# Delta rule of a recurrent mixer on quarter-array blocks: one block for the tiles, one solve of eight units, a scan with joined query and key products, and a merge in token rows

## The reference, cut to what matters

```python
def run_gdn(q, k, v, g, beta, s0, emit):        # chunks of 64 tokens, heads of 128
    gc = jnp.cumsum(g, axis=-1)
    decay = jnp.exp(jnp.where(lower, gc[..., :, None] - gc[..., None, :], -jnp.inf))
    lmat = jnp.where(strict, einsum(k * beta, k) * decay, 0.0) + jnp.eye(CHUNK)
    rhs = concatenate([v * beta, k * beta * exp(gc)])
    u0, kcd = triangular_solve(lmat, rhs, unit_diagonal=True)
    kd = k * exp(gc_last - gc);  gl = exp(gc_last)
    attn = einsum(q, k) * decay;  qd = q * exp(gc)     # latent chunks only
    def step(s):
        u = u0_i - kcd_i @ s
        s_new = s * gl_i + kd_i.T @ u
        o = qd_i @ s + attn_i @ u                      # latent chunks only
y_gdn = head_rmsnorm(o_forward + o_backward, gdn_norm_w) * silu(z)
y_gla = head_rmsnorm(o_gla, gla_norm_w) * silu(g)
```

## Time and profile before

| | us |
|---|---|
| median of 3 runs | 2598.92 (2583.86 to 2602.16) |
| the profiled execution, device time | 2598.43 |
| its span | 2596.6 |

### The profile page before, as it was taken

How to read it: one execution, slowest core, us unless ns; L and a number is a source line. 1 busy time by engine, 2 the same in 40 slices (tenths; PEclk the granted TensorE clock), 3 DMA queues, 4 the chain that set the end, 5 groups by cost and what they waited for, 6 DMA issues and landing times. The chain is left out here.

```text
span 2596.6 us, 34628 instructions
## 1 busy us (share of the span) xinstructions
PE 2331.0 (90%) x14344; PEld 2015.8 (78%) x14344; DVE 1617.0 (62%) x2449; ACT 860.4 (33%) x1198; POOL 0.2 (0%) x4
## 2 busy tenths in 40 slices
PE   4999999989999999899958995878799987878998
PEld 2998998866799899669957885878589976345997
DVE  1878877254687887468754556676467734444545
ACT  2344443034434544243435322320143411112442
POOL 0000000000000000000000000000000000000000
PEclk9999999979999999999979997988699989789999
DMA  8765886200688688258841120000077743001551
GB/s 324 292 247 190 324 323 260 84 15 29 256 327 313 259 323 323 85 218 327 321 168 49 65 84 31 1 1 1 0 281 304 304 157 130 1 0 65 212 197 53
DMA packets 65739, 450.64 MB, mean 174 GB/s; under 512 B 8023, under 2 KB 9240, under 8 KB 12696
## 3 DMA queue, kind: packets, MB, share of 16 engines
q1 hardware_dynamic: 65624, 449.09, 45.2%
HBM read 448.01 MB, written 1.05 MB: 173 GB/s over the span
## 5 line engine op out<-in xcount | busy, mean ns | idle before, releaser
L460 PEld LDWEIGHTS banks<-ffn_h_split,ffn_weights_split 128*128 128x128 f32 x7392 | 906.5, 194 | 25.3 <-DVE ffn_weights_split L533 11.7
L460 PE MATMUL banks<-ffn_h_split,ffn_weights_split 128*128 128x256 f32 x7392 | 910.4, 285 | 17.5 <-DVE ffn_h_split L550 17.4
L678 DVE TENSOR_TENSOR ffn_weights_split<-weight_ring,ffn_weights_split 128x2048 fp32r<-128x2048 f32 x224 | 511.9, 2287 | 236.7 <-ACT ffn_weights_split L593 236.5
L593 ACT CAST ffn_weights_split<-weight_ring 128x2048 fp32r<-128x2048 f32 x224 | 425.5, 1903 | 169.0 <-PE banks L475 168.8
L475 PE MATMUL banks<-ffn_weights_split,ffn_hidden_split 128*128 128x512 f32 x1512 | 354.7, 390 | 0.0
L475 PEld LDWEIGHTS banks<-ffn_weights_split,ffn_hidden_split 128*128 128x128 f32 x1512 | 279.9, 188 | 55.5
L641 DVE CUSTOM_DVE_ANT_0 weight_ring<-weight_ring,first_arena,cols 128x1024 f32<-128x1024 f32 x200 | 245.3, 1279 | 0.0
L564 ACT ACTIVATE ffn_arena<-banks 128x256 f32<-128x256 f32 x154 | 59.1, 384 | 526.8 <-PE banks L460 526.8
L796 PE MATMUL banks<-h,weight_ring 128*128 128x256 f32 x544 | 123.5, 392 | 7.6 <-PEq L84 7.6
L796 PEld LDWEIGHTS banks<-h,weight_ring 128*128 128x128 f32 x544 | 107.2, 197 | 24.0 <-issue 8.4
L627 DVE TENSOR_TENSOR ffn_arena<-banks,ffn_arena 128x256 f32<-128x256 f32 x154 | 64.7, 420 | 49.0 <-ACT ffn_arena L564 49.0
(11 more groups left out here) (327 smaller groups left out, 2431.0 us busy)
## 6 DMA issues: line engine op xcount, KB each, us to landing
weight_ring<-in_weights SPq DMA_DIRECT2D x407, 1024.0 KB, 4.9
first_arena<-in_norm_rows SPq DMA_DIRECT2D x12, 512.0 KB, 6.7
first_arena<-in_c_rows SPq DMA_DIRECT2D x4, 512.0 KB, 5.7
h<-in_ctx SPq DMA_DIRECT2D x1, 1024.0 KB
first_arena<-in_x SPq DMA_DIRECT2D x1, 1024.0 KB
first_arena<-in_ctx_rows SPq DMA_DIRECT2D x1, 1024.0 KB
x<-in_x_rows SPq DMA_DIRECT2D x1, 1024.0 KB
recurrent_arena<-in_ctx SPq DMA_DIRECT2D x1, 1024.0 KB, 4.9
```

Of the source, the lines that this page charges most:

```text
L460: last = nc.tensor.matmul(bank[:, half * T:half * T + T], w[:, x, sl], hs[:, k, y, :], start=(k == 0 and x + y == 0), stop=(k == DT - 1 an ...
L593: nc.scalar.copy(wsplit[:, c % S, 0, :], raw).then_inc(self.split_hi.sem, 1)
L678: nc.vector.tensor_tensor(wsplit[:, c % S, 1, :], core.wbuf[:, (self.first + at(c)) % NSLOT, :], wsplit[:, c % S, 0, :].bitcast(F32), ALU. ...
```

## The change

- GLA merge: the sums over the head are made with one column of ones, so they stand with tokens on partitions (128x8 for all heads). Root and reciprocal are taken of 128x8, spread over the features by matmuls (`rstd` broadcast against the identity), and applied as two products of 128x512.
- `gdn_tiles` does factors and all four tiles in one block, with two sets of banks and two sets of rows.
- `gdn_solve` runs once, on eight units. X, W and the products are stored as 128x256: the 64x64 blocks of a head's two chunks lie one above the other, and every product is eight matmuls of 64x64 blocks, those of chunk one in the upper left quarter of the array, those of chunk two in the lower right. Units follow each other in slots; `product(n)` and `change(n - 3)` alternate. X and W of a unit share one bank and one subtraction. The keys scaled for the state (`kte`) are made by ScalarE here.
- `gdn_scan`: keys and queries of a latent chunk stand side by side (`kq`), so one product gives both `kcd @ s` and `qd @ s`; `attn @ u` is added in the same bank, with tokens on partitions. The scaling L2032 is gone. Context steps have an additional matmul of 128x256 with the identity whose result nobody reads. The output of the two directions is put together in token rows, normed there, turned by eight transposes, and gated. `ab_merge` is gone.

```diff
             pe.wait_ge(state.sem, state.base + 16)
             for hd in range(NG):
                 pe.wait_ge(msquared.sem, msquared.base + hd + 1)
-                last = nc.tensor.matmul(core.ps[hd // 2][:, (hd % 2) * T:(hd % 2) * T + T], core.ones[:, :],
-                                        b["msq"][:, hd, :], start=True, stop=True)
+                for t in range(TT):
+                    last = nc.tensor.matmul(core.ps[0][:, 2 * hd + t:2 * hd + t + 1], b["msq"][:, hd, t * P:t * P + P],
+                                            core.ones[:, 0:1], start=True, stop=True)
+            last.then_inc(sums.sem, 1)
+            pe.wait_ge(msteps.sem, msteps.base + 1)
+            for hd in range(NG):
+                for t in range(TT):
+                    last = nc.tensor.matmul(core.ps[1 - hd // 2][:, (hd % 2) * T + t * P:(hd % 2) * T + t * P + P],
+                                            b["rstd"][:, 2 * hd + t:2 * hd + t + 1].broadcast_to([P, P]), core.ident[:, :],
+                                            start=True, stop=True)
                 if hd % 2:
-                    last.then_inc(sums.sem, 1)
+                    last.then_inc(spread.sem, 1)
...
+            act.wait_ge(sums.sem, sums.base + 1)
+            nc.scalar.activation(b["root"][:, :], core.ps[0][:, 0:2 * NG], ACT.Sqrt, scale=1.0 / P, bias=core.rms_eps)\
+                .then_inc(mact.sem, 1)
...
+            step, z = Steps(dve, msteps), b["lg"]
+            dve.wait_ge(mact.sem, mact.base + NG + 1)
+            step(nc.vector.reciprocal(b["rstd"][:, :], b["root"][:, :]))
             for hd in range(NG):
-                dve.wait_ge(mact.sem, mact.base + NG + hd + 1)
-                step(nc.vector.reciprocal(msq[:, hd, :], msq[:, hd, :]))
-                step(nc.vector.tensor_tensor(msq[:, hd, :], o_of(hd), msq[:, hd, :], ALU.mult))
-                step(nc.vector.scalar_tensor_tensor(z[:, hd, :], msq[:, hd, :], core.col("gla_norm_w")[:, 0:1], z[:, hd, :],
-                                                    ALU.mult, ALU.mult))
+                last = nc.vector.scalar_tensor_tensor(z[:, hd, :], o_of(hd), core.col("gla_norm_w")[:, 0:1], z[:, hd, :],
+                                                      ALU.mult, ALU.mult)
+            step(last)
+            for a in range(2):
+                dve.wait_ge(spread.sem, spread.base + a + 1)
+                pair = z[:, 2 * a:2 * a + 2, :].rearrange("p a t -> p (a t)")
+                nc.vector.tensor_tensor(pair, pair, core.ps[1 - a][:, :], ALU.mult)
...
+UNITS = 2 * TK
+LEVELS = 6
+SLOTS = (LEVELS - 1) * UNITS
+LAG = 3
...
+                if n >= 2:
+                    pe.wait_ge(l_s.sem, l_s.base + first[n - 1])
...
+            copies(0)
+            for n in range(TK):
+                decays(n)
+                if n + 1 < TK:
+                    copies(n + 1)
+                for m in range(first[n], first[n + 1]):
+                    _, kind, d = jobs[m]
+                    act.wait_ge(ex_s.sem, ex_s.base + m + 1)
+                    src = gc[:, 0, :, :] if kind == "l" else b["ngc"][:, :, :]
+                    for h in range(NG):
...
+            def product(s):
+                u, lv = s % UNITS, s // UNITS + 1
+                pe.wait_ge(masked.sem, masked.base + s + 1)
+                if lv == 1:
+                    pe.wait_ge(w_ready.sem, w_ready.base + u + 1)
+                else:
+                    pe.wait_ge(updated.sem, updated.base + s - UNITS + 1)
+                for r, c in blocks:
+                    last = nc.tensor.matmul(core.ps[u][r, c], o[r, s % 4, c], w_of(u)[r, c], start=True, stop=True)
+                last.then_inc(p_ready.sem, 1)
+            def change(s):
+                u, lv = s % UNITS, s // UNITS + 1
+                pe.wait_ge(p_copied.sem, p_copied.base + s + 1)
+                for r, c in blocks:
+                    last = nc.tensor.matmul(core.ps[u][r, c], x_of(u)[r, c], pm[r, s % 4, c], start=True, stop=True)
+                if lv < LEVELS - 1:
+                    for r, c in blocks:
+                        last = nc.tensor.matmul(core.ps[u][r, W + c.start:W + c.stop], pm[r, s % 4, c], x_of(u)[r, c],
+                                                start=True, stop=True)
+                last.then_inc(wp_ready.sem, 1)
...
+            for n in range(SLOTS + 2 + UNITS):
+                if n < SLOTS:
+                    product(n)
+                if LAG <= n < SLOTS + LAG:
+                    change(n - LAG)
+                if 0 <= n - SLOTS + 2 < UNITS:
+                    values(n - SLOTS + 2)
+                if 0 <= n - SLOTS - 2 < UNITS:
+                    keys(n - SLOTS - 2)
...
+            for n in range(SLOTS + 4 + UNITS):
+                if n < SLOTS:
+                    act.wait_ge(p_ready.sem, p_ready.base + n + 1)
+                    nc.scalar.copy(pm[:, n % 4, :], core.ps[n % UNITS][:, 0:W]).then_inc(p_copied.sem, 1)
+                if n < len(scaled):
+                    t, d, h = scaled[n]
+                    nc.scalar.activation(b["kte"][t][d][:, h, :], b["ktm"][:, t, h, :], ACT.Identity,
+                                         bias=0.0, scale=b["ed"][:, t, 4 * d + h:4 * d + h + 1])
+                if 0 <= n - SLOTS + 1 < UNITS:
+                    out_values(n - SLOTS + 1)
+                if 0 <= n - SLOTS - 3 < UNITS:
+                    out_keys(n - SLOTS - 3)
...
+            def scale_keys(u):
+                if u >= 2:
+                    dve.wait_ge(kcd_ready.sem, kcd_ready.base + u - 1)
...
+            for s in range(SLOTS + 2 + UNITS):
+                if s + 5 < SLOTS:
+                    mask(s + 5)
+                if s < SLOTS:
+                    update(s)
+                if 0 <= s - SLOTS + 7 < UNITS:
+                    scale_values(s - SLOTS + 7)
+                if 0 <= s - SLOTS + 5 < UNITS:
+                    scale_keys(s - SLOTS + 5)
...
+                        if n >= TT:
+                            last = nc.tensor.matmul(bank_of(d, i)[:, h * P:h * P + P],
+                                                    b["kq"][:, n - TT, 4 * d + h, 2 * lo:2 * lo + P], s[:, 4 * d + h, :],
+                                                    start=(h == 0), stop=True, skip_group_check=True)
+                        else:
+                            last = nc.tensor.matmul(bank_of(d, i)[lo:lo + CK, h * P:h * P + P],
+                                                    b["kc"][:, n, 4 * d + h, lo:lo + CK], s[:, 4 * d + h, :],
+                                                    start=True, stop=True)
...
+                if i < LATENT:
+                    nc.tensor.matmul(core.ps[6][:, 0:T], core.ident[:, :],
+                                     b["kc"][:, 0, 0:2, :].rearrange("p h t -> p (h t)"), start=True, stop=True)
+                else:
+                    for d in range(2):
+                        n, lo = chunk(d, i)
                         for h in range(NG):
+                            last = nc.tensor.matmul(bank_of(d, i)[CK - lo:2 * CK - lo, h * P:h * P + P],
+                                                    b["att"][n - TT][lo:lo + CK, 4 * d + h, :],
+                                                    u[lo:lo + CK, d, h * P:h * P + P], start=False, stop=True,
+                                                    skip_group_check=True)
+                        last.then_inc(at_s[d].sem, 1)
+            for h in range(NG):
+                if h == 0:
+                    pe.wait_ge(scaled_s.sem, scaled_s.base + 2)
+                for t in range(TT):
+                    last = nc.tensor.transpose(core.ps[6 + h // 2][:, (h % 2) * T + t * P:(h % 2) * T + t * P + P],
+                                               o[:, t, h * P:h * P + P], core.ident[:, :])
+                last.then_inc(turned_s.sem, 1)
...
+            nc.scalar.activation(b["warm"][:, :], core.one, ACT.Sqrt)
+            for i in range(LATENT, LATENT + 2):
+                for d in range(2):
+                    n, lo = chunk(d, i)
+                    r = slice(CK - lo, 2 * CK - lo)
+                    act.wait_ge(at_s[d].sem, at_s[d].base + i - LATENT + 1)
+                    nc.scalar.copy(o[r, n - TT, :], bank_of(d, i)[r, :]).then_inc(out_s[d].sem, 1)
+            for t in range(TT):
+                act.wait_ge(sum_s.sem, sum_s.base + 2)
+                for h in range(NG):
+                    last = nc.scalar.activation(b["junk"][:, t, h * P:h * P + P], o[:, t, h * P:h * P + P], ACT.Square,
+                                                accum_out=b["ss"][:, t, h:h + 1])
+                last.then_inc(sq_s.sem, 1)
+            act.wait_ge(sq_s.sem, sq_s.base + 2)
+            nc.scalar.activation(b["root"][:, :, :], b["ss"][:, :, :], ACT.Sqrt, scale=1.0 / P, bias=core.rms_eps)\
+                .then_inc(root_s.sem, 1)
...
+                    if i + 1 < STEPS:
+                        dve.wait_ge(du_s[d].sem, du_s[d].base + i + 1)
```

(14 more changed lines are left out.)

523 lines of the change are left out of this document (221 added, 302 removed).

## The result

| | us |
|---|---|
| median after, 4 runs | 2479.65 (2479.59 to 2484.94) |
| median before, 4 runs beside them | 2591.39 (2581.23 to 2602.16) |
| ratio | 0.958, 95% interval 0.954 to 0.961 |
| profiled execution, before and after | 2598.43 and 2479.59 |

The account below looks back on a forecast made before the run. PE was taken as the bound, busy 90% of the span; savings of 7.8 (GLA merge), 1.8 (tiles), 61.6 (solve) and 34.0 (scan and merge) summed to 105.2, so 2598.4 - 105.2 = 2493 us, range 2475 to 2535.

Parts of the forecast that it names:

- Slots: Solve: 32 slots of 1.40 us and 8 last-level ones of 0.93, at 29 ns a record, 52.2 us.
- the 38 ns of the 128-column row: Solve: alternative record spacing, from quarters with 128 columns taking 0.61 us for 16; at 38 ns, 16 us more.
- Head: Solve's start: VectorE makes and masks X, last unit's turn on PE ends at 9.7 us; low clock adds 2 us.
- outputs, waits and end: Solve's end: outputs 14.1 us, changing between quarters and whole array 2, waits behind scale_keys 6.7, copy and meeting 1.6.
- rival 1: The solve stays at 1.2 GHz, slots taking 97.8 us for 54.2 and outputs 10 more: 2547 us; chance 0.12.
- the two reasons: Solve: slow stretches had half the rows idle or 128-column loads against 64 streamed; here both row halves work, loads equal streams.
- Rival 2: The solve's quarters, writing one bank, do not overlap: slots 141 us more, 2652 us, slower by 2%; chance 0.08.
- Rival 3: PE's queue is not fed at 29 ns in the solve: 2509 to 2545 us, 2552 by the skill page; chance 0.10.
- Tiles: Tiles block: VectorE work unchanged, with waits for spread, copy and exponentials: 39.5 us, 1.8 less; bounds 27 and 43.
- its third: Tiles: the last of three forecast VectorE waits, 1.3 us, after those of 5.0 and 4.8.
- Merge: Behind the scan: squares 4 us, root and reciprocal 0.9, products 1.4, transposes and gates 4.9, small waits 1.6; 12.8 us.
- Scan: Scan: context steps with cold start 21.6 us, latent steps 5.2 each if the clock is high; 44.1 us.

Follow-up runs that it names:

- whole-blocks run: Changed kernel with the solve's products and changes as four 128x128 matmuls in place of eight of 64x64: 2525.56 us, solve 134.1 us.
- run without lag: Changed kernel with the solve's change(n) right behind product(n) on PE, LAG 0 in place of 3: 2506.68 us, solve 112.9 us.
- feature-major run: Changed kernel with latent steps turned back to state and delta as weights, keys times state alone; output not the reference's: 2478.75 us, scan 45.30 us.
- scan by direction: Feature-major kernel with each direction's queries, update and attention product one behind the other on PE in latent steps: 2500.17 us, scan 62.4 us.
- keys scaled later: Changed kernel with scale_keys two places later in VectorE's order at the solve's end: 2468.6 us, solve 78.4 us.
- last kernel: Changed kernel with scale_keys later, ScalarE's next-tile copies later, and the state's memset moved to the solve's head: median 2458.90 us, ratio to before 0.949.

## Why the prediction was right, and where it was off

**The mechanism** held in each block, and 2479.65 lies 13.3 under the forecast, near the lower end of its range. The blocks account for it: 191.1 forecast, 176.6 measured, 14.5 less; 0.8 more outside them. All five blocks came out shorter, so the forecast erred to one side: 0.5 in the GLA merge, 4.3 in the tiles, 2.8 in the solve, 2.5 in the scan, 4.5 in the merge.

**Slots: exact.** 1.40 us against 1.40, from the row with 64 columns streamed; the 38 ns of the 128-column row was the wrong relative. The whole-blocks run confirms the price of the alternative, and the run without lag confirms what the order hides. Head: 8.36 where I had 9.7 and 2 for a cold start; the clock rose at 1615.73, still in the head, so the slots had no cold start. What is left behind the head and 52.2 of slots is 25.0, to 24.4 forecast for outputs, waits and end. That this fits is partly luck: the waits took 4.9 us (1.73, 1.73 and 1.40) for 6.7, and a stretch of 3.4 us at 0.50 that the forecast did not have gave it back.

**Rivals 1 and 2** are out by the 29 ns and the clock of 1.00. Of the two reasons that the forecast gave against rival 1, one fell alone: the feature-major run loads 128 columns for 64 streamed, and its latent steps stayed at 1.00. Rival 2 had the Trainium skill for it, "TensorEngine Tiling (Array Packing)", section "Restrictions and Gotchas", by which row tiles do not use one PSUM bank at once. The trace disagrees for diagonal quarters, which write different partitions of one bank: 29 ns a record for 50 us. The forecast argued this and had no row for it.

**Rival 3** is out: 96 instructions in 1.40 us, no gap. The Trainium skill, "TensorE: Matmul & The Clock Gate", section "Wait — 56ns, not 53.3ns?", has some 62 ns per MATMUL for a sequencer without hardware decode; 29 ns a record is less than half of that, so this is not the case that ran here.

**Tiles: mis-sized, 35.25 for 39.5.** Two waits stood where the walk put them, 4.00 and 3.74 for 5.0 and 4.8, and its third, of 1.3, is not in the trace. The largest part came from the start. I priced the first spread cold, 3.75 us, but the clock was still 1.00 behind the short GLA merge. Timeline of PE after:

```profile
1575.32 2.02 PE L1759 MATMUL banks<-recurrent_arena 128*128 128x128 f32 x16 [1.22 <-PEq L84]
1577.27 0.69 PE L1767 MATMUL banks<-recurrent_arena 128*64 128x64 f32 x16
```

1.95 us, and the first factor came 6.3 us after the start, not 8.9. Together these are 6.0 us; what stands between them took 1.7 more than the walk had.

**Merge: mis-sized, 8.31 for 12.8.** Squares come 0.30 us apart, not the 0.5 that I took from rows of other lines: 1.6 of the 4.5. Transposes and gates ran in 3.4 for 4.9 (1742.08 to 1745.47), root and reciprocal in 0.5 for 0.9; the rest are small waits.

**Scan: mis-sized, 41.57 for 44.1.** Latent steps took 5.4 for 5.2. The four context steps took 18.8 (5.5, 4.6, 4.4 and 4.3) for 18.0 and a cold start of 3.6; the cold start was the term at fault, since the clock stood at 0.50 for 3.4 us only (1697.65 to 1701.07). The forecast wrote "if the clock is high" and did not ask what would hold it there. That was its weakest step, and that it came out right was luck.

The runs, taken one behind the other, split the 31.8 us of the scan so: 17.1 is the order of the two directions in the old form, some 13.5 of it the clock; 3.7 is the form in token rows with the joined product (2.0 of it the join); 11.0 is the rest. That rest was not taken apart; L2032 out of each step is in it, and so is the clock, 0.73 over the scan by direction and 0.67 over the old one. Taken the other way round, the order is worth 1.8 and the form 19.0: what holds the clock up cannot be put down to one of them.

## What to carry to other kernels

Price small matmuls by the row of the trace with the same streamed length and the same share of the array, and hide what stands between them with other units: here the quarters would have lost over half of their gain to one copy. Before counting on the clock, look for rows of records that leave half of the array idle; two independent chains that use opposite row halves belong next to each other, group by group. Here that order was worth 1.8 us in one form of the products and 17.1 in the other, where the clock fell without it. And when a queue holds work for later ahead of work that is due, move it back: two such moves, and a memset made ahead of the block that waits for it, gave another 19 us.

## What was not expected of the hardware

- Records of the next row half start before the last of this one, against program order, by about three records (L1894 at 1640.44 ahead of L1887 at 1640.49, 1640.55 and 1640.61).
- Column halves one behind the other, eight records each, ran at 78 ns a record for 128 streamed columns, the whole array at 124.
- The clock fell to 0.50 behind a stretch in which PE was busy for 27.29 of 27.30 us, and stayed at 1.00 in slots of which every instruction used a quarter of the array.
- The first context steps of the scan ran at 0.50 for 10.20 us with PE busy throughout (keys scaled later), and at 1.00 in the last kernel, with the same instructions.
